# Down product, first column group: nine units of seven products, and eight low parts formed by GpSimd transfers that add

## What is computed

```
u = rmsnorm(h, pre_ffn_g[i])
ff = (jax.nn.silu(u @ w_gate[i]) * (u @ w_up[i])) @ w_down[i]
h = h + rmsnorm(ff, post_ffn_g[i])
```

## Time and profile before

| | us |
|---|---|
| median of 3 runs | 1076.89 |
| lowest and highest | 1075.95 and 1077.07 |
| the execution that was profiled | 1076.7 |
| its span in the profile | 1074.8 |

### The profile page before, as it was taken

One profiled execution on the slowest core, in us unless ns is written; L12 is line 12 of the kernel. 1 busy time (PEld: TensorE's weight loads), 2 busy tenths in 40 slices (PEclk: granted clock), 3 DMA queues, 4 the chain that ended last, 5 costly groups with the idle time before them and its releaser, 6 DMA issues. The chain is left out here.

```text
span 1074.8 us, 15382 instructions
## 1 busy us (share of the span) xinstructions
PE 1064.1 (99%) x5745; PEld 922.1 (86%) x5745; DVE 891.3 (83%) x1083; ACT 599.2 (56%) x736; POOL 27.3 (3%) x46
## 2 busy tenths in 40 slices
PE   9999999999999999999999999999999999999996
PEld 8999999999888888888888888888888888888885
DVE  5699987646646787898998998988989899988887
ACT  6554454736545565555565655655655555655553
POOL 4000101101000000000000000000000000000000
PEclk9999999999999999999999999999999999999999
DMA  8655535444386476766756656657667655566665
GB/s 273 208 176 167 172 106 160 136 143 138 111 309 213 141 263 186 225 188 191 225 174 195 216 182 210 201 178 229 186 190 219 226 197 196 194 209 219 200 202 191
DMA packets 113208, 208.06 MB, mean 194 GB/s; under 512 B 9184, under 2 KB 46496, under 8 KB 111856
## 3 DMA queue, kind: packets, MB, share of 16 engines
q1 hardware_dynamic: 111952, 201.49, 58.6%
q10 hardware_dynamic: 608, 4.20, 1.0%
q0 software_dynamic: 576, 1.40, 0.4%
HBM read 202.86 MB, written 4.19 MB: 193 GB/s over the span
## 5 line engine op out<-in xcount | busy, mean ns | idle before, releaser
L554 ACT ACTIVATE w_hi<-raw 128x1024 fp32r<-128x1024 f32 x322 | 337.9, 1059 | 260.4 <-PE ps L1713 149.6
L907 DVE TENSOR_TENSOR w_lo<-raw,w_hi 128x1024 fp32r<-128x1024 f32 x322 | 390.4, 1226 | 82.5 <-ACT w_hi L554 81.9
L1711 PE MATMUL ps<-w_hi,uf 128*128 128x512 f32 x524 | 205.3, 392 | 0.1
L1713 PE MATMUL ps<-w_hi,uf 128*128 128x512 f32 x524 | 204.1, 389 | 0.0
L1712 PE MATMUL ps<-w_lo,uf 128*128 128x512 f32 x524 | 203.9, 389 | 0.0
L1375 PE MATMUL ps<-u,w_hi 128*128 128x272 f32 (+1 forms) x544 | 158.8, 292 | 0.0
L1377 PE MATMUL ps<-u,w_hi 128*128 128x272 f32 (+1 forms) x544 | 155.9, 287 | 0.0
L1378 PE MATMUL ps<-u,w_lo 128*128 128x272 f32 (+1 forms) x544 | 155.7, 286 | 0.0
L838 ACT CAST t_hi<-tx 128x1024 fp32r<-128x1024 f32 x92 | 96.3, 1052 | 65.9 <-DVE tx L1200 54.6
L1713 PEld LDWEIGHTS ps<-w_hi,uf 128*128 128x128 f32 x524 | 98.4, 188 | 20.6
L1711 PEld LDWEIGHTS ps<-w_hi,uf 128*128 128x128 f32 x524 | 98.4, 188 | 20.5 <-issue 0.5
(11 more groups left out here) (271 smaller groups left out, 1469.7 us busy)
## 6 DMA issues: line engine op xcount, KB each, us to landing
raw<-in_w_gate SPq DMA_DIRECT2D x176, 256.0 KB, 2.9
raw<-in_w_up SPq DMA_DIRECT2D x176, 256.0 KB, 3.5
raw<-in_w_down SPq DMA_DIRECT2D x88, 512.0 KB, 4.2
raw<-in_w_in SPq DMA_DIRECT2D x72, 512.0 KB, 3.6
raw<-in_w_out SPq DMA_DIRECT2D x32, 512.0 KB, 4.4
arena<-in_x SPq DMA_DIRECT2D x2, 1024.0 KB, 5.9
arena<-in_x ACTq DMA_DIRECT2D x2, 1024.0 KB, 8.5
out<-h2rows SPq DMA_DIRECT2D x2, 1024.0 KB, 5.5
```

The lines of the kernel that those rows point to most:

```text
L554: act.activation(w_hi[:, slot, :], raw[:, slot, :], ACT.Copy).then_inc(hi_done, 1)
L907: dve.tensor_tensor(w_lo[:, slot, :], raw[:, slot, :], hi_view(w_hi[:, slot, :]), ALU.subtract).then_inc(lo_done, 1)
L1711: pe.matmul(o, a[0], b[0], start=start, stop=False)
L1713: return pe.matmul(o, a[1], b[0], start=False, stop=stop)
```

## The change

The first column group gets the order `PPPPZPZPZPZPZPZPZPZZPP`: nine units of seven products, 13 plain ones. The sums of the left operand are made at chunks 4, 6, 10, 14, ... 34 in place of 4, 10, 12, 18, ... 36.

For eight chunks (`ADDED_CH`: 10, 14, 18, 22, 26, 30, 34 and 40, each the first chunk of a plain unit) VectorE no longer makes the low part. ScalarE writes the negated and rounded value into `w_lo` (`minus_hi`), and GpSimd issues a transfer from `raw` to `w_lo` that adds what it reads to what lies there (`accum_op=ALU.add`). Of such a chunk TensorE does the eight matmuls with high weights first, then waits for the transfer and does the four with the low part. SyncE loads the next chunk into the slot only when the transfer has landed.

```
-    SUM_AT = {4: 11, 10: 12, 12: 13, 18: 14, 22: 15, 24: 16, 28: 17, 32: 18, 36: 19}
+    SUM_AT = {4: 11, 6: 12, 10: 13, 14: 14, 18: 15, 22: 16, 26: 17, 30: 18, 34: 19}
...
-    ROUND = ["PPPPPPPP"] + ["PPZPZPZP"] * (NFG - 1) + ["PPPPZPPZPPZPPZPZPZPZPP", "PPPZPZPZPZPZPZPZPZPZPP"]
+    ADDED_CH = (10, 14, 18, 22, 26, 30, 34, 40)
+    ROUND = ["PPPPPPPP"] + ["PPZPZPZP"] * (NFG - 1) + ["PPPPZPZPZPZPZPZPZPZZPP", "PPPZPZPZPZPZPZPZPZPZPP"]
...
+    def lo_by_dve(q):
+        return q + 1 - sum(1 for a in ADDED if a <= q)
+    def lo_by_dma(q):
+        return 16 * sum(1 for a in ADDED if a <= q and (a - q) % WSLOTS == 0)
...
-                sp_eng.wait_ge(lo_done, q - WSLOTS + 1)
+                if q - WSLOTS in ADDED_NO:
+                    sp_eng.wait_ge(lo_added[q % WSLOTS], lo_by_dma(q - WSLOTS))
+                else:
+                    sp_eng.wait_ge(lo_done, lo_by_dve(q - WSLOTS))
...
+            for i, q in enumerate(ADDED):
+                slot = q % WSLOTS
+                pool.wait_ge(neg_done, i + 1)
+                pool.dma_start(w_lo[:, slot, :].bitcast(F32), raw[:, slot, :], accum_op=ALU.add).then_inc(lo_added[slot], 16)
...
+            def minus_hi(q):
+                slot = q % WSLOTS
+                act.activation(w_lo[:, slot, :], raw[:, slot, :], ACT.Copy, scale=-1.0).then_inc(neg_done, 1)
...
+                if q in ADDED_NO:
+                    pe.wait_ge(hi_done, q + 1)
+                    for m, j in quarters:
+                        for h in range(2):
+                            pe.matmul(quarter(g, m, j), left(g, kt, m)[h], right(q, j)[0], start=ch == 0 and h == 0, stop=False)
+                    pe.wait_ge(lo_added[q % WSLOTS], lo_by_dma(q))
+                    for m, j in quarters:
+                        mm = pe.matmul(quarter(g, m, j), left(g, kt, m)[0], right(q, j)[1], start=False, stop=ch == chs - 1)
+                    return mm
```

More of the change, by code:

```diff
@@ L153, in place_of @@
         return g, ch, TURNS[g][ch // 2]
+    ADDED = [BEGIN[NFG] + ch for ch in ADDED_CH]
+    ADDED_NO = {q: i for i, q in enumerate(ADDED)}
+    def lo_by_dve(q):
+        return q + 1 - sum(1 for a in ADDED if a <= q)
+    def lo_by_dma(q):
+        return 16 * sum(1 for a in ADDED if a <= q and (a - q) % WSLOTS == 0)
     def landed(q):
@@ L347, in build_trunk @@
             sem(n) for n in ("rows_done", "turned", "h2_hi", "h2_lo", "h2_sq", "r2c_done"))
+        neg_done, lo_added = sem("neg_done"), [sem(f"lo_added{s}") for s in range(WSLOTS)]
         silu_done, p_done, f_hi, f_lo = (sem(n) for n in ("silu_done", "p_done", "f_hi", "f_lo"))
@@ L864, in _ @@
                         split(q)
+                        if q in ADDED_NO:
+                            minus_hi(q)
                         if z is not None:
@@ L1301, in _ @@
                         inner_product(g - 1)
-                    if z is None:
+                    if z is None and q not in ADDED_NO:
                         split(q)
-                    elif ch % 2:
+                    elif z is not None and ch % 2:
                         weight_sums(q, z)
@@ L1725, in plain_products @@
                 kt, chs = 2 * d + ch % 2, 2 * len(ROUND[g])
-                pe.wait_ge(lo_done, q + 1)
                 if g >= NFG:
                     pe.wait_ge(f_lo, kt // 4 + 1)
+                if q in ADDED_NO:
+                    pe.wait_ge(hi_done, q + 1)
[6 more added lines that the diff above has]
+                    return mm
+                pe.wait_ge(lo_done, lo_by_dve(q))
                 for m, j in quarters:
@@ L1755, in seven_products @@
                 three(m1, left(g, 2 * d, 0), right(q, 0), begin, end).then_inc(chunks_used, 1)
-                pe.wait_ge(lo_done, q + 2)
+                pe.wait_ge(lo_done, lo_by_dve(q + 1))
                 three(quarter(g, 0, 0), left(g, 2 * d + 1, 0), right(q + 1, 0))
```

## The result

The changed kernel takes 1082.72 us (median of 6 runs, 1080.59 to 1084.06) against 1076.54 us before (median of 6 as well): a ratio of 1.0058, 95% interval 1.0047 to 1.0069. It is 6.2 us slower. The profiled execution took 1084.06 us, the most of the six, with a span of 1082.2 us, 7.4 us over the span of before.

A forecast was written before the change was run, and what follows sets the result against it. TensorE, busy 20.00 of 20.00 us, was taken as the bound. Six fewer matmuls (-1.4 us) and the ring's stall (+5.0 us) summed to +3.6 us, giving 1080.5 us; range 1075.2 to 1094.5 us.

The forecast's parts named there:

- the ring: Chunks 10, 14, ... 34 share one slot: load, high part, negated copy, transfer; late turns stall TensorE 5.0 us; chance 0.46.
- What is removed: In the first column group's down product, two plain units become units of seven: 6 fewer matmuls, gaining 1.36 us.
- VectorE: Per Z and P pair it needs 10.02 us with one low part, 11.2 with two, against TensorE's 10.2: costs nothing.
- X: Time of an adding transfer from GpSimd's issue to landing: taken as 5.7 us, bounds 4.4 to 7.7.
- 7X - 34.9: Whole stall of TensorE over the first transfer and six following turns, where above zero: 5.0 us at X = 5.7.
- One turn takes 5.4 + X: Load 3.1 us, high part and negated copy 2.0, hand-overs 0.3, plus X, against TensorE's 10.2 us per pair.
- Chunk 40 has another slot and comes after four chunks of units of seven: nothing.: At the end of the first column group, the transfer of chunk 40 was to cost no stall.
- (a): Rival: the transfer is hidden, X up to 5, no stall, 1075.5 us; chance 0.39.
- (b): Rival: slow transfer, doubled reading meeting a burst of four loads; X 7.7 or more, 1094.5 us or more; chance 0.12.
- (c): Rival: VectorE becomes the bound, its 10.02 us a pair growing beyond 10.2; 0.2 to 2.4 us, so 1078; no chance given.

The follow-up runs named there:

- e5: The changed kernel with transfers that copy instead of adding, no two units of seven in a row, and chunk 38 in place of 40: 1074.54 us.
- e1: The changed kernel with no added chunks: nine units of seven, all low parts by VectorE, no transfers: 1080.31 us.
- e9: The changed kernel with no added chunks and no two units of seven in a row, all low parts by VectorE: 1078.50 us.
- e4: The changed kernel with the eight transfers copying instead of adding, all waits the same: 1077.87 us.
- e10: The changed kernel with no two units of seven in a row and eight adding transfers at chunks 10, 14, ... 38: 1079.72 us.
- e6: The kernel before, seven units of seven and no transfers, reordered so that two units of seven stand in a row: 1079.07 us.
- e2: The changed kernel with added chunks 10, 15, 18, 23, 26, 31, 34, 40, so the transfers use two slots by turns: 1087.94 us.
- e3: The changed kernel with transfers adding another buffer, so SyncE's loads wait only for the negated copy and not for the transfer: 1089.24 us.
- e12: e10 with only the left 512 columns of each added chunk by negated copy and transfer, VectorE making the right 512: 1074.99 us.
- e7: As e3, with transfers adding another buffer, but SyncE's loads wait for the transfer as in the changed kernel: 1081.91 us.

## Why the prediction was right, and where it was not

The direction and the range were right: slower, 1082.7 us in 1075.2 to 1094.5, and the ring that it named is in the trace. The size was low, +3.6 against +6.2 us in the median and +7.4 in the profiled span, and the ring is only about half of it.

- **What is removed.** 1.36 us, as counted: 5745 - 5739 = 6 matmul records, and e5, where nothing waits, has 1.3 us less between the first and the last matmul of the down product (228.3 against 229.6 us) and 2.2 us less in the median.
- **VectorE.** The 11.2 against 10.2 us without transfers is borne out by e1 and e9, where each late unit is late by 0.7 to 0.9 us, and by the 11.14 us from one to the next in e9; that its pace with one low part fits, by e5, where no wait is left.
- **X.** Taken as 5.7, measured 5.2, in bounds of 4.4 to 7.7. The parts were close: copy 3.6 for my 4.5, second reading 1.6 for 1.6. Why the copy was too dear no run separates: the row of 4.4 us came from the crowded start, and from an input of the kernel and not from SBUF. GpSimd's own share was 0.85 us and not 0.53; 0.53 is what the copy in e4 takes. On the two pages cited: the rule that an addition costs its second reading (the Trainium skill, Collectives: The Full Stack, "The bandwidth ceiling: the fold count and why AG ≠ RS ≠ AR"), which the page states of a collective's reduce step, agrees with e4 against the changed kernel, 1.6 us for 512 KB. The fit that gives an estimate of 3.2 us (the Trainium skill, DMA: Bandwidth & Descriptors, "Anatomy of one DMA — SWDGE (gpsimd) path") is near e4's 3.6 and e5's 3.9 for a copy, and 2 us short for an addition.
- **The ring.** Forecast 5.0 us of waiting in chunks 10 to 34, measured 4.9. That they agree is luck. With the measured X of 5.2 the prediction's own 7X - 34.9 gives 1.5 us. Its "One turn takes 5.4 + X" was too small: beside X a turn took 6.0 us, since loads at the head of their burst took 3.2 to 4.8 us rather than always 3.1, and that made up for the smaller X (turns of 11.1 us forecast, 11.4 measured). At the two ends the errors went the other way: TensorE came to the transfer of chunk 10 at 866.0 and not 865.6, and the transfer of chunk 34 took 4.5 us. And 4.9 is of the slowest of six executions; the same seven turns cost 3.2 us in e10. In the median, 6.2 + 1.4 - 4.0 leaves an estimate of 3.6 us for the ring, if the end of the group costs there what it costs in the profile.
- **The step that failed** is "Chunk 40 has another slot and comes after four chunks of units of seven: nothing." I looked at the end of the group only for transfers, and did not ask what two units of seven in a row do to each other. They share the buffer `tx`, and that costs 2.2 us (e6), and through ScalarE's order another 1.8 us at chunk 40 (read from the trace; no run keeps a transfer at chunk 40 without the pair), in sum the 4.0 us by which the profiled execution exceeds the forecast (7.5 against 3.6). The wait of VectorE on `t_used` stands in `weight_sums`; the row that would have shown it does not exist before, because a plain unit lay between any two.
- **The rivals.** (a) would not have paid even with a hidden transfer: with the pair it gives e4's 1077.9, not 1075.5. (b) didn't happen in the changed kernel, and does in e2 and e3, for the reason that it gave, loads beside the transfer. (c) did not happen with the transfers in place.

What stays open: e5's and e12's medians are 0.8 and 1.3 us lower than their matmuls and waits account for; the beginning of the down product alone differs by 1.0 us between profiled executions (836.0 to 837.0 us), so single traces don't settle it. Nor did any run take away the ring and leave the transfer as it was: e2 and e3 loosen it and make X longer, e4 and e12 make X shorter and also read less. That the ring binds in the changed kernel rests on its trace: SyncE waits for the transfer, ScalarE for the load and TensorE for the transfer, turn after turn.

## What to carry to other kernels

A transfer that stands between a load and the next load of the same buffer makes a ring; add up its whole turn and hold it against the period of the engine that sets the time, for latency that is free once is paid at every turn. When two heavy units move next to each other, look for every buffer that they share with only one copy before counting what their number saves. And the time of a transfer is not its own: here one wait of SyncE changed it from 7 to 5 us, so taking that wait away made the kernel 7 us slower (e3 against e7), the most of it at the one transfer that met five loads.

## What the runs showed of the hardware

- An adding transfer of 512 KB inside SBUF, issued by GpSimd, lands in 4.5 to 6.5 us (the changed kernel, e7, e10) with further loads of weights held back, in 6.1 to 8.9 us (median 7.1, e3) with them running; a copy of the same size in 3.5 to 5.1 (e4, e5); an addition of 256 KB in 4.0 to 5.3 (e12). Half the size saves only 0.8 of the 5.2 us.
- GpSimd is busy 0.85 us for issuing an addition of either size (0.95 for the first), 0.53 us for a copy (e4).
- VectorE's subtractions beside these transfers are no longer than before: the twelve L933 of the changed kernel that run during one have a mean of 1224 ns, L933 over the program 1226, and L907 had 1226.
- In some executions TensorE's granted clock fell after the wait of 2.2 us behind the pair (e1, e2, e7), and not in others with the same wait (the changed kernel, e4, e6). In e1 the window at 940 to 957 us has 0.90 of the clock, and the matmuls behind the wait start 0.43 us apart, twice the usual distance, the lower of the two levels (1.2 GHz), until about 946 us:

```profile
940.00:957.00 17.00, 15.10 (x60) 12.20 (x60) 13.78 (x13) 9.07 (x10) 0.00 (x0) 0.90 0.64 219
```

In the changed kernel's profiled execution the same window has 1.00. What this costs shows in e4's ten executions: the five with a mean clock of 0.996 took 1078.3 to 1078.8 us, the five with 0.998 or 0.999 took 1076.5 to 1077.4. It does not explain the spread of the changed kernel's times, 3.5 us against 1.4 before: its executions of 1084.06, 1084.00 and 1080.59 us all have 0.998 or 0.999. There the waits for transfers differ, as the 4.9 and 3.2 us of the same seven turns in two traces suggest; that is inferred.
